# One layer of a gated-mixer decoder with mixture of experts: where the routing weights are applied, when the last down weights are requested, and which engine adds the token rows

## The chip, the cores and the metric

The kernel runs on one core of one Trainium2 chip. TensorE (PE) multiplies, VectorE (DVE), ScalarE (ACT) and GpSimd (POOL) do the rest, and SyncE (SP) requests nearly all transfers between HBM and SBUF; GpSimd requests those with a list of row numbers. The metric is the device time of one launch in microseconds (us), the median of several runs.

## The reference, cut to what matters

There are 512 tokens of 1024 channels, in float32. A first part (four gated mixers) is not touched by the change. The part that is:

```python
xn = rms_norm(x, ffn_norm_g)
# group = argmax of 4 group logits; two best of the 8 experts of that group
combine[token, expert] = p_group * top_p / sum(top_p)      # two non-zero values per token
for e in range(32):
    hid = silu(xn @ w_expert_gate[e]) * (xn @ w_expert_up[e])   # 1024 -> 256
    out = out + combine[:, e:e+1] * (hid @ w_expert_down[e])    # 256 -> 1024
return rms_norm(x + out, final_norm_g)
```

So each token gets its own row, plus two expert rows, each times a routing weight, and is then normalised.

## The kernel before

**Slots.** The 32 experts are handled in pairs. A pair fills 128 partitions: 64 slots for each of its two experts, and a slot holds one (token, expert) pair. Small tables made by TensorE from one-hot matrices `hot` give for each slot the row in which its result is kept (`slots`), its token (`toks`) and its token's norm factor (`rslot`). `weight_products` makes a table of the same kind for the routing weights, but of six columns only. There are 17 turns: the first four pairs (turns 0 to 3), three further pairs, two turns for the fullest expert, which gets more than 64 slots (`OVER`, `PART`), and the other eight pairs. Which pair holds the fullest expert is only known at run time, and so `exchange_columns` in turn 1 moves the columns of the tables about on VectorE, and `overflow_hits` then makes the matrices `hot` anew for the expert's slots beyond the 64th. These are chains of small operations, each of which waits for the one before.

**A turn.** TensorE multiplies 128 slots by the gate and up weights of both experts (line 2020, 64 matmuls), ScalarE and VectorE make `hid` from it (lines 1003 and 1552), TensorE transposes that (line 2040) and multiplies by the down weights (line 2061, 16 matmuls, two banks of PSUM `b` = 0 and 1). ScalarE and VectorE copy the banks to `ye` (lines 1021 and 1573), and GpSimd scatters the 128 rows to `y_dram`, which has two rows for each token (line 703).

**Weights.** Each turn needs six units of 1 MB. They lie in a ring of 20 slots; SyncE requests unit w as soon as unit w-20 has been used (`wait_reuse`), in the order of the turns. The last two units (the down weights of turn 16, `last_down`) are left out of this order: SyncE first waits for the 15 scatters, requests the results, and then the two units, in halves by columns, of which TensorE waits for the first with `d_half`.

**The end.** The last two turns (`KEPT`) do not go through `y_dram`. Their rows are split in two parts `yeh` and `yel` (ScalarE line 1012, VectorE line 1563; `w_kept` holds the routing weights of these two turns), and TensorE adds them to the tokens by a product with the one-hot matrices `pick` (`kept_products`, line 1977). The rows of the 15 other turns come back from `y_dram` in `load_results`, for each of the four tiles of 128 tokens two transfers of 0.5 MB (`yt[t][:, 0]` and `yt[t][:, 1]`, in the slots of `ring_z` and `ring_x`). VectorE multiplies them by the routing weights `cw` and adds the token's own row `x2` (`gather_results`, two operations per tile). For tiles 0 and 1 TensorE adds this to the sum in PSUM (`add_sum`, line 1985), for tiles 2 and 3 VectorE adds PSUM to it (`added`, line 1638). Then ScalarE squares and sums (line 1039), VectorE scales (`scaled`) and SyncE writes out. The tiles go in the order 3, 0, 2, 1 through TensorE (`SUMMED`) and 0, 3, 1, 2 through the norm (`NORMED`).

If an expert got more tokens than the two turns for it hold, the branches under `most > SLOT` run; with these inputs they do not.

## Time and profile before

| | |
|---|---|
| median of 3 runs | 736.96 us (734.79 to 739.46) |
| profiled execution | 735.92 us, of which the span of the trace is 734.2 us |
| mean granted TensorE clock | 0.975 of full speed |
| TensorE busy | 694.5 us (95%) |
| VectorE, ScalarE, GpSimd busy | 362.5, 252.2, 83.2 us |
| moved by DMA | 163.67 MB, mean 223 GB/s |
| turns 0 to 16 of the experts | from 478.6 to 718.5 us of the span |

The shares are averages over stages with different limits. In the part without experts (up to some 478 us) TensorE sets the time; in the expert part one has to look, stretch by stretch, whether TensorE or the stream of weights does; in the last 15 us neither is busy all the time.

### The profile page before, as it was taken

The numbers are of one execution on the slowest core, as the hardware profiler recorded it, in microseconds if no ns is written. First come the engines' busy times: TensorE is split into PE (matmuls) and PEld (weight loads), VectorE is DVE, ScalarE is ACT, GpSimd is POOL, SyncE is SP. The second block draws the span as 40 slices with busy tenths as digits, with TensorE's granted clock in tenths as the row PEclk, the third lists the DMA queues.
The fourth block names the chain that finished last, engine by engine and source line by source line (L and its number), as shares of the span: only waits on it lengthen the run. The fifth ranks groups of instructions, "written<-read, shape, count | busy, mean of one in ns | idle before, by whom it ended". The sixth has DMA issues, their size and how long they took to land.

```text
span 734.2 us, 9954 instructions
## 1 busy us (share of the span) xinstructions
PE 694.5 (95%) x3919; PEld 514.9 (70%) x3919; DVE 362.5 (49%) x700; ACT 252.2 (34%) x413; POOL 83.2 (11%) x117
## 2 busy tenths in 40 slices
PE   5999999999999999999999999699999999998975
PEld 4888987877777777788888888565555555554453
DVE  5378996356667767656456205635221212110246
ACT  7332135466767667544243211200010111110104
POOL 2001922000010101100002000201212121111000
PEclk9999999999999999999999999689999999998998
DMA  6523244221111122493405798489999999999982
GB/s 232 172 61 113 66 115 144 72 71 63 56 59 58 61 66 73 140 381 123 129 1 229 296 364 339 167 332 390 392 417 421 405 419 420 419 420 417 367 327 118
DMA packets 61153, 163.67 MB, mean 223 GB/s; under 512 B 7986, under 2 KB 39807, under 8 KB 49068
## 3 DMA queue, kind: packets, MB, share of 16 engines
q1 hardware_dynamic: 55468, 150.71, 54.3%
q0 software_dynamic: 5632, 12.25, 4.4%
q8 instruction: 33, 0.54, 0.3%
q14 instruction: 20, 0.16, 0.1%
HBM read 155.16 MB, written 15.99 MB: 233 GB/s over the span
## 4 chain that ended last, share of the span: by engine, by line
PE 82%; DMA 8%; DVE 4%; SPq 3%; ACT 2%; issue 1%; POOLq 0%; ACTq 0%; DVEq 0%
PE psum L1657 30%; PE psum L1753 12%; PE psum L2020 11%; PE psum L1932 6%; PE psum L2061 6%; DMA ring_z<-in_w_expert_up 4%; PE psum L1765 3%; SPq L495 2%; DMA ring_p<-in_w_expert_down 2%; PE psum L1778 2%; PE psum L1808 1%; DMA y_dram<-ye,slots 1%; PE psum L1843 1%; PE psum L1831 1%; PE psum L1891 1%
## 5 line engine op out<-in xcount | busy, mean ns | idle before, releaser
L1657 PE MATMUL psum<-xh,wh 128*128 128x512 f32 x256 | 99.9, 390 | 1.5 <-DVE xl L1049 1.5
L1657 PE MATMUL psum<-xh,wl 128*128 128x512 f32 x256 | 99.6, 389 | 0.0
L1657 PE MATMUL psum<-xl,wh 128*128 128x512 f32 x256 | 99.6, 389 | 0.0
L1052 DVE TENSOR_TENSOR wl<-raw,wh 128x1280 fp32r<-128x1280 f32 (+4 forms) x37 | 71.8, 1945 | 24.8 <-ACT wh L757 9.0
L1049 DVE SCALAR_TENSOR_TENSOR hid<-psum,rslot,act_g 128x256 f32<-128x256 f32 x17 | 8.2, 484 | 106.8 <-ACT act_g L1003 106.8
L1003 ACT ACTIVATE act_g<-psum,rslot 128x256 f32<-128x256 f32 x17 | 8.0, 473 | 149.9 <-PE psum L2020 149.9
L1657 PEld LDWEIGHTS psum<-xh,wh 128*128 128x128 f32 x256 | 48.1, 188 | 11.6 <-DVE xl L1049 1.7
L1657 PEld LDWEIGHTS psum<-xh,wl 128*128 128x128 f32 x256 | 48.1, 188 | 10.1
L1657 PEld LDWEIGHTS psum<-xl,wh 128*128 128x128 f32 x256 | 48.1, 188 | 9.8
L1753 PE MATMUL psum<-xh,wh 128*128 128x512 f32 x128 | 51.7, 404 | 0.0
L1753 PE MATMUL psum<-xh,wl 128*128 128x512 f32 x128 | 50.1, 391 | 0.0
L1753 PE MATMUL psum<-xl,wh 128*128 128x512 f32 x128 | 49.9, 390 | 0.0
L1049 DVE SCALAR_TENSOR_TENSOR sg<-cu,ch,sg 128x512 f32<-128x512 f32 x60 | 48.8, 883 | 0.0
L1573 DVE COPY ye<-psum 128x512 f32<-128x512 f32 x15 | 10.4, 692 | 60.7 <-PE psum L2061 60.7
L2020 PE MATMUL psum<-ring_h,xT 128*64 128x256 f32 x224 | 37.4, 398 | 3.1 <-DMA ring_h<-in_w_expert_up 3.1
L2020 PE MATMUL psum<-ring_w,xT 128*64 128x256 f32 x240 | 40.2, 379 | 0.0
L703 POOL DMA_INDIRECT y_dram<-ye,slots x15 | 15.1, 1008 | 172.9 <-DVE ye L1573 158.3
L2020 PE MATMUL psum<-ring_e,xT 128*64 128x256 f32 x160 | 31.3, 401 | 3.1 <-DMA ring_z<-in_w_expert_up 3.1
L2020 PEld LDWEIGHTS psum<-ring_h,xT 128*64 128x64 f32 x224 | 22.9, 143 | 14.2 <-issue 5.6
L2020 PE MATMUL psum<-ring_z,xT 128*64 128x256 f32 x128 | 31.8, 412 | 0.1
L2020 PEld LDWEIGHTS psum<-ring_w,xT 128*64 128x64 f32 x240 | 24.3, 137 | 8.9 <-issue 1.7
L1268 DVE TENSOR_TENSOR gp<-gs,psum 128x512 f32<-128x512 f32 x16 | 11.0, 685 | 36.6 <-PE psum L1657 35.8
(365 smaller groups left out, 1484.4 us busy)
## 6 DMA issues: line engine op xcount, KB each, us to landing
raw<-in_w_gate SPq DMA_DIRECT2D x16, 1024.0 KB, 6.3
raw<-in_w_in SPq DMA_DIRECT2D x9, 1024.0 KB, 5.8
ring_w<-in_w_expert_up SPq DMA_DIRECT2D x8, 1024.0 KB, 20.1
ring_w<-in_w_expert_gate SPq DMA_DIRECT2D x7, 1024.0 KB, 21.1
ring_h<-in_w_expert_gate SPq DMA_DIRECT2D x7, 1024.0 KB
ring_h<-in_w_expert_up SPq DMA_DIRECT2D x7, 1024.0 KB
ring_h<-in_w_expert_down SPq DMA_DIRECT2D x6, 1024.0 KB
ring_e<-in_w_expert_down SPq DMA_DIRECT2D x6, 1024.0 KB, 30.2
```

The costliest lines, as they stand in the source:

```text
L495: sp_e.dma_start(raw_slots[slot], weights(*units_of(c)[w], found)).then_inc(ring_full[slot], 16)
L703: pool.indirect_dma_start(out=y_dram[:, :], out_offset=bass.IndirectOffsetOnAxis(ap=slots[n, p], axis=0), in_=ye[n, s, :], in_offset=None, ...
L1049: return dve.scalar_tensor_tensor(out=out_, in0=a, scalar=s, in1=b, op0=o0, op1=o1)
L1052: return dve.tensor_tensor(dst, src, hi.bitcast(F32), ALU.subtract)
L1268: dve.tensor_tensor(gp[:, m, :], gs[:, m, :], branch_bank(cg, m)[:, :], ALU.mult).then_inc(S["gate_free"], 1)
L1657: last = nc.tensor.matmul(dst, a, b, start=start and n == 0, stop=stop and n == len(seq) - 1)
L1753: last = nc.tensor.matmul(bank[6 + n % 2][:, :], a[:, c, f], b[:, c, :], start=c == 0 and q == 0, stop=c == KC - 1 and q == 2)
L1765: last = nc.tensor.matmul(bank[4 + n % 2][:, :], a[:, j, f], b[g][:, j, :], start=j == 0 and q == 0, stop=j == BJ - 1 and q == 2)
L1778: last = nc.tensor.matmul(gate_bank(0, m)[:, :], a[:, c, f], b[:, c, :], start=c == 0 and q == 0, stop=c == KC - 1 and q == 2)
L1932: last = nc.tensor.matmul(bank[t][:, :], x_[:, t, c, :], w_[:, b, c, :], start=c == 0 and m == 0, stop=c == KC - 1 and m == 2)
L2020: last = nc.tensor.matmul(bank[2][half, m * FE:(m + 1) * FE], xT[:, k, half], w[h][:, k, :], start=k == 0 and m == 0, stop=k == KC - 1, sk ...
L2061: last = nc.tensor.matmul(bank[5 + b][half, :], hidT[:, m, half], w_d[h][:, m, b * T:(b + 1) * T], start=m == 0, stop=m == FE // P - 1)
```

## The change

Four things change. First, the routing weights are applied per slot when the down product leaves PSUM: the table of weights gets all 32 columns and becomes `wslot`, `slot_weights` copies it in turn 0, `exchange_columns` and `overflow_column` do for it what they do for `rslot`, and `weight_products` runs a second time in turn 1. `kept_weights` and `w_kept` go. Second, the last two down units are requested in their turn by the loop over all units, as whole units, ahead of the results. Third, GpSimd adds `x2` to the first of the two result rows of each tile (`add_tokens`), and VectorE adds the second (`add_rows`), one plain addition each. Fourth, the tiles go in the order 0, 2, 1, 3 through both TensorE and the norm; the square root's table on ScalarE is loaded in turn 16.

```diff
-        SUMMED, NORMED = (3, 0, 2, 1), (0, 3, 1, 2)
+        SUMMED = (0, 2, 1, 3)
 ...
-            last_down = [unit_no(0, LAST, half, 2) for half in range(2)]
-            for w in range(NU, last_down[0]):
+            for w in range(NU, UNITS0):
 ...
             load_results()
-            for w in last_down:
-                wait_reuse(0, w)
-            for b in range(2):
-                for w in last_down:
 ...
+            def add_tokens(n):
+                for t in range(NT):
+                    pool.wait_ge(y_in[t], 32 + 32 * n)
+                    pool.tensor_tensor(yt[t][:, 0, :], yt[t][:, 0, :], x2[:, t, :], ALU.add).then_inc(S["y_add"], 1)
+
             expert_pass(0)
+            add_tokens(1)
 ...
+                    if isinstance(c, int) and i == LAST:
+                        act.preload_act_table(ACT.Sqrt)
 ...
-                        act.activation(ye[:, s, 0:T], bank[5][:, :], ACT.Copy).then_inc(S["y_a"], 1)
+                        act.activation(ye[:, s, 0:T], bank[5][:, :], ACT.Copy, scale=wslot[:, column(c, i)]).then_inc(S["y_a"], 1)
 ...
+            def slot_weights(n):
+                dve.wait_ge(S["w_ps"], n)
+                for h in range(2):
+                    half = slice(h * SLOT, (h + 1) * SLOT)
+                    dve.tensor_copy(wslot[half, 0:NPAIR], bank[7][half, 448:448 + NE].rearrange("p (e h) -> p h e", h=2)[:, h, :]).then_inc(S["rs_ready"], 1)
 ...
-                exchanged(moved[:, FIXED:], rslot[:, FIXED:NPAIR], rslot[:, OVER:OVER + 1], gap[:, FIXED:])
-                one_column(bank[7][:, 384:384 + NE], emask)
-                st.mark(dve.tensor_copy(rslot[:, OVER:OVER + 1], rs[:, 13, 0:1]))
-                one_column(bank[7][:, 384:384 + NE], fmask)
-                st.link(dve.tensor_copy(rslot[first, NPAIR:NPAIR + 1], rs[first, 13, 0:1]))
+                for table, at in ((rslot, 384), (wslot, 448)):
+                    exchanged(moved[:, FIXED:], table[:, FIXED:NPAIR], table[:, OVER:OVER + 1], gap[:, FIXED:])
+                    one_column(bank[7][:, at:at + NE], emask)
+                    st.mark(dve.tensor_copy(table[:, OVER:OVER + 1], rs[:, 13, 0:1]))
+                    one_column(bank[7][:, at:at + NE], fmask)
+                    st.link(dve.tensor_copy(table[first, NPAIR:NPAIR + 1], rs[first, 13, 0:1]))
 ...
-            def gather_results(n, tiles):
-                for t in tiles:
-                    dve.wait_ge(y_in[t], 32 + 32 * n)
-                    for j, b in enumerate((x2[:, t, :], yt[t][:, 0, :])):
-                        stt(yt[t][:, 0, :], yt[t][:, j, :], cw[:, j, t:t + 1], b, ALU.mult, ALU.add).then_inc(S["comb_in"], 1)
+            def add_rows(n, t, done="comb_in"):
+                dve.wait_ge(y_in[t], 32 + 32 * n)
+                dve.wait_ge(S["y_add"], NT * (n - 1) + t + 1)
+                dve.tensor_tensor(yt[t][:, 0, :], yt[t][:, 0, :], yt[t][:, 1, :], ALU.add).then_inc(S[done], 1)
 ...
                     if isinstance(c, int) and i == 1:
                         exchange_columns()
-                        kept_weights()
                         overflow_hits()
 ...
-                    if isinstance(c, int) and i == LAST:
-                        gather_results(1, range(1))
 ...
-                                gather_results(1, range(1 + 2 * b, 3 + b))
+                                add_rows(1, b)
 ...
-                        dve.tensor_copy(ye[:, s, T:2 * T], bank[6][:, :]).then_inc(S["y_b"], 1)
+                        dve.tensor_scalar(ye[:, s, T:2 * T], bank[6][:, :], wslot[:, column(c, i)], None, ALU.mult).then_inc(S["y_b"], 1)
 ...
             expert_pass(0)
+            add_rows(1, 2)
 ...
-            added(3)
-            scaled(0)
-            scaled(3)
-            added(2)
-            scaled(1)
-            scaled(2)
+            scaled(0)
+            dve.wait_ge(S["comb_in"], 3)
+            added(2)
+            add_rows(1, 3, "comb")
+            dve.wait_ge(S["comb"], 2)
+            added(3)
+            for t in SUMMED[1:]:
+                scaled(t)
 ...
                     if isinstance(c, int) and i == 1:
                         pe.wait_ge(S["hot_ready"], NT + 1)
                         slot_products()
+                        weight_products()
                         norm_products(2)
```

VectorE in turn 1, from the last lookup in `slots` on. Before (`w_pairs` is the six-column table, `rc` a scratch table, L1468 the start of `overflow_hits`):

```order
L1457 TENSOR_SCALAR slots<-rs 64x1 [waits dve_step]
L1436 TENSOR_SCALAR rc<-rslot 128x12 [waits dve_step]
L1437 TENSOR_TENSOR rc<-rc 128x12 [waits dve_step]
...
L1463 COPY rslot<-rs 64x1 [waits dve_step]
L1512 COPY w_pairs<-psum 64x3 [waits dve_step,w_ps]
L1512 COPY w_pairs<-psum 64x3
L1436 TENSOR_SCALAR rc<-w_pairs 128x2 [waits dve_step]
L1437 TENSOR_TENSOR rc<-rc 128x2 [waits dve_step]
L1438 TENSOR_TENSOR w_pairs<-w_pairs,rc 128x2 [waits dve_step]
L1515 COPY w_kept<-w_pairs 128x2 [waits dve_step]
L1468 TENSOR_SCALAR rank<-rank 128x8 [waits dve_step]
L1344 TENSOR_SCALAR hot<-slot_no,rank 128x128 [waits rs_ps,dve_step]
```

Now, from the end of the same treatment of `rslot`:

```order
L1474 COPY rslot<-rs 64x1 [waits dve_step]
L1446 TENSOR_SCALAR rc<-wslot 128x12 [waits dve_step]
L1447 TENSOR_TENSOR rc<-rc 128x12 [waits dve_step]
L1448 TENSOR_TENSOR wslot<-wslot,rc 128x12 [waits dve_step]
L1452 TENSOR_TENSOR rc<-psum,rc 128x32 [waits dve_step]
L1453 TENSOR_REDUCE rs<-rc 128x1 [waits dve_step]
L1472 COPY wslot<-rs 128x1 [waits dve_step]
L1452 TENSOR_TENSOR rc<-psum,rc 128x32 [waits dve_step]
L1453 TENSOR_REDUCE rs<-rc 128x1 [waits dve_step]
L1474 COPY wslot<-rs 64x1 [waits dve_step]
L1479 TENSOR_SCALAR rank<-rank 128x8 [waits dve_step]
L1347 TENSOR_SCALAR hot<-slot_no,rank 128x128 [waits rs_ps,dve_step]
```

Between `rslot` and `rank` six small operations have become nine, all ahead of the matrices `hot`.

TensorE in turn 1, between the two halves of the turn. Before, and then now (L1958 and L1965 are `norm_products`, L1973 is `weight_products`):

```order
L1910 MATMUL psum<-rv,hot 128x32 [waits hot_ready]
L1910 MATMUL psum<-rv,hot 128x32 x7
L1958 MATMUL psum<-rro,hot 128x32 [waits rs_in]
L1958 MATMUL psum<-rro,hot 128x32 x7
```

```order
L1917 MATMUL psum<-rv,hot 128x32 [waits hot_ready]
L1917 MATMUL psum<-rv,hot 128x32 x7
L1973 MATMUL psum<-rvw,hot 128x32 [waits rs_in]
L1973 MATMUL psum<-rvw,hot 128x32 x7
L1965 MATMUL psum<-rro,hot 128x32 [waits rs_in]
L1965 MATMUL psum<-rro,hot 128x32 x7
```

Eight matmuls have come in, behind the wait for `hot` and ahead of the transposes of `hid`.

VectorE from the last `hid` on (turn 16). Before:

```order
L1049 SCALAR_TENSOR_TENSOR ring_z<-ring_z,cw,x 128x1024 [waits x0]
L1049 SCALAR_TENSOR_TENSOR ring_z<-ring_z,cw 128x1024 [waits comb_in]
L1049 SCALAR_TENSOR_TENSOR hid<-psum,rslot,act_g 128x256 [waits silu,comb_in]
...
L1049 SCALAR_TENSOR_TENSOR ring_x<-ring_x,cw 128x1024 [waits comb_in]
L1049 SCALAR_TENSOR_TENSOR yel<-psum,w_kept,yeh 128x512 [waits y_hi,comb_in]
L1049 SCALAR_TENSOR_TENSOR ring_x<-ring_x,cw,x 128x1024 [waits x3]
L1049 SCALAR_TENSOR_TENSOR ring_x<-ring_x,cw 128x1024 [waits comb_in]
L1049 SCALAR_TENSOR_TENSOR yel<-psum,w_kept,yeh 128x512 [waits y_hi,comb_in]
```

Now:

```order
L1052 SCALAR_TENSOR_TENSOR hid<-psum,rslot,act_g 128x256 [waits silu]
L1528 TENSOR_TENSOR ring_z<-ring_z 128x1024 [waits y_add,x0]
L1052 SCALAR_TENSOR_TENSOR yel<-psum,wslot,yeh 128x512 [waits y_hi]
L1528 TENSOR_TENSOR ring_z<-ring_z 128x1024 [waits y_add,x1]
L1052 SCALAR_TENSOR_TENSOR yel<-psum,wslot,yeh 128x512 [waits y_hi]
L1528 TENSOR_TENSOR ring_x<-ring_x 128x1024 [waits y_add,x2s]
```

Eight additions with a product have become four additions (that of tile 3 comes later, after `added(2)`), and each waits for GpSimd's `y_add`.

## Rows read from the trace of the kernel before

**Rows 1.** Windows: stretch, its length, busy time (instructions) by engine, TensorE clock, DMA share, GB/s.

```profile
515.00:520.00 5.00, 5.00 (x48) 3.18 (x45) 1.07 (x3) 0.28 (x1) 1.29 (x2) 1.00 0.91 321
520.00:525.00 5.00, 4.45 (x25) 2.02 (x25) 1.68 (x3) 1.17 (x3) 0.00 (x0) 1.00 1.03 420
...
684.00:688.00 4.00, 3.81 (x38) 3.08 (x38) 0.69 (x1) 0.00 (x0) 1.02 (x1) 1.00 1.00 416
...
692.00:696.00 4.00, 3.47 (x18) 1.46 (x19) 1.61 (x3) 0.88 (x2) 0.00 (x0) 1.00 0.67 259
```

**Rows 2.** Timeline of SyncE's requests: start, us, line, what, count.

```profile
519.78 0.33 SPq L495 DMA_DIRECT2D ring_h<-in_w_expert_gate  x1
...
670.32 2.58 SPq L495 DMA_DIRECT2D ring_h<-in_w_expert_up  x1
694.13 1.76 SPq L572 DMA_DIRECT2D ring_z<-y_dram  x4
...
698.20 6.31 SPq L584 DMA_DIRECT2D ring_p<-in_w_expert_down  x4
```

**Rows 3.** Who waited for whom, 640 us on: total, times, longest.

```profile
PE psum L2020 <- DMA ring_z<-in_w_expert_up: 3.1, 1, 3.1
```

**Rows 4.** Timeline of TensorE at the end; idle time before and its releaser in brackets.

```profile
700.18 8.81 PE L2020 MATMUL psum<-ring_h,xT 128*64 128x256 f32 x64 [3.07 <-DMA ring_h<-in_w_expert_up]
...
713.19 1.94 PE L2061 MATMUL psum<-ring_p,hidT 128*64 128x512 f32 x8 [0.63 <-DMA ring_p<-in_w_expert_down]
716.59 1.94 PE L2061 MATMUL psum<-ring_p,hidT 128*64 128x512 f32 x8 [1.46 <-DMA ring_p<-in_w_expert_down]
```

**Rows 5.** The chain that ended last, at the end: start, us, what.

```profile
720.44 3.66 PE psum L1977 x16
724.09 1.72 PE psum L1985 x4
...
726.77 1.12 ACT ring_z L1039 x2
728.44 1.28 DVE ring_z L1049
729.83 1.28 DVE ring_x L1049
```

**Rows 6.** Timeline of VectorE in turn 1.

```profile
498.96 0.23 DVE L1436 TENSOR_SCALAR rc<-rslot 128x12 f32<-128x12 f32 x1
...
500.59 0.14 DVE L1463 COPY rslot<-rs 64x1 f32<-64x1 f32 x1
...
501.92 0.17 DVE L1515 COPY w_kept<-w_pairs 128x2 f32<-128x2 f32 x1
```

**Rows 7.** The chain that ended last, in turns 0 and 1.

```profile
488.11 1.78 PE psum L1966 x16
...
505.11 1.80 PE psum L1958 x16
506.91 0.45 PE psum L2040 x2
```

**Rows 8.** Timeline of VectorE at the end.

```profile
702.54 1.28 DVE L1049 SCALAR_TENSOR_TENSOR ring_z<-ring_z,cw,x 128x1024 f32<-128x1024 f32 x1 [3.91 <-DMA ring_z<-y_dram]
...
719.70 0.75 DVE L1049 SCALAR_TENSOR_TENSOR yel<-psum,w_kept,yeh 128x512 fp32r<-128x512 f32 x1 [0.42 <-DVE ring_x L1049]
```

**Rows 9.** Line 572, the requests of the results: time from request to landing.

```profile
DMA to landing us min/median/max: 4.8/9.3/12.9
```

**Rows 10.** Timeline of GpSimd, two additions of the mixer part.

```profile
76.67 1.39 POOL L642 TENSOR_TENSOR axb<-axb,gs 128x512 f32<-128x512 f32 x1
...
87.04 3.43 POOL L642 TENSOR_TENSOR axb<-axb,gs 128x512 f32<-128x512 f32 x1
```

**Rows 11.** Timeline of VectorE beside the second of these.

```profile
87.03 2.28 DVE L1052 TENSOR_TENSOR wl<-raw,wh 128x2048 fp32r<-128x2048 f32 x1
```

**Rows 12.** Tile sg on VectorE: duration in ns, least, median, most.

```profile
L1049 DVE SCALAR_TENSOR_TENSOR sg<-cu,ch,sg x60: 737/744/1789, 43.4 to 112.3; 128x512 f32<-128x512 f32 x60
```

More of the change, by code:

```diff
@@ L1555, in expert_pass @@
                             x_out(E + 1, b)
+                    if isinstance(c, int) and i == 0:
+                        slot_weights(1)
+                        dve.wait_ge(S["rs_ready"], 4)
                     if isinstance(c, int) and i >= LAST - 1:
```

78 lines of the change are left out of this document (34 added, 44 removed).

## The prediction, made before the changed kernel was run

> **What bounds the kernel now.** I read four views in this order: the windows, to see stretch by stretch whether TensorE or the DMA is full; the waits, for who waits for a transfer; the chain that ended last; the timelines around the two places that the change touches, turn 1 and the end.
>
> The windows [rows 1] show two regimes. In the stretch 515 to 520 us the DMA is busy 0.91 of the time. From 520 to 688 us every stretch shows a share of 1.00 or more (24 stretches of 5 us to 640, twelve of 4 us to 688; the first and the last are shown). SyncE's request at 519.78 us takes 0.33 us, that at 670.32 us 2.58 us [rows 2]: the first finds an empty queue and had waited for a buffer, the second finds a full queue. So from 520 us on the stream of weights sets the pace, and TensorE, which is ahead by what the ring holds, runs into it twice, for 3.1 us each, before turns 14 and 16 [rows 3, 4]. **What counts for the expert part is when the stream gets the request of 519.78 us, and that hangs on TensorE in turns 0 to 2.** The two waits of 3.1 us are no reserve for a delay there, since they are waits for transfers that would be late by the same amount.
>
> At the end, SyncE requests nothing between 672.9 us (670.32 + 2.58) and 694.13 us, then the results, and the last down weights from 698.20 us on [rows 2]. The DMA share falls to 0.67 from 692 to 696 us [rows 1]. TensorE waits for the down weights before each half, 0.63 and 1.46 us, and is done with them at 718.53 us [rows 4]. A relay of TensorE, ScalarE and VectorE over four tiles follows; the last scaling ends at 731.1 us [rows 5], and the span ends 3.1 us later, with the last output.
>
> **The change, part by part.**
>
> *VectorE in turn 1.* The small operations on `rslot` run from 498.96 to 500.73 us [rows 6]; the same on `wslot` is new: 1.77 us. What goes is the work on the kept weights, from there to 502.09 us [rows 6]: 1.36 us. The matrices `hot` are ready 0.4 us later; I take 0.5, as one semaphore step is added too.
>
> *TensorE in turn 1.* It waits for `hot`, then runs slot and norm products, then transposes `hid` at 506.91 us [rows 7]; the chain goes straight from the norm products to the transposes, so `hid` is not what they wait for. A second set of weight products comes in between. That set, six columns wide, took 1.78 us in turn 0, and the norm products, already 32 wide, 1.80 us [rows 7]: the width costs nothing in turn 0, and the second set costs 1.8 us. The transposes start 0.5 + 1.8 = **2.3 us later**, and with them all of turns 1 and 2, the end of the gate and up product of turn 2, and the request of 519.78 us. Queued behind that request are all later weights, so the stream ends 2.3 us later. Bounds: nothing, if the stream had work left at 519.78; 2.8, if each of the nine new operations, and not only the first, takes the 0.23 us of rows 6. I take 2.3, as the request of 0.33 us speaks for an empty queue.
>
> *The rest of turns 0 to 15.* `slot_weights` are two small copies in turn 0, between `hid` and the down product, which VectorE waits for there; the three further operations of `overflow_column` stand likewise in turn 2 ahead of a `hid` that TensorE sets. The copies out of PSUM get a factor; with a factor and a second input they take 0.75 us [rows 8], and TensorE needs the bank again only a turn later. I cost this at nothing; the cover is VectorE's idle time, and without it three small operations cost 0.6 us.
>
> *The last down weights in their turn.* They are requested from 672.9 us on, right behind the weights of turn 16, whose landing starts that turn at 700.2 us [rows 4]. At 420 GB/s [rows 1] 2 MB take 5.1 us: they land at 705.3, before TensorE asks for them. Both waits for them go. TensorE is ready for them at 713.19 - 0.63 = 712.6, and two halves of 1.94 us [rows 4] end at 716.4 us in place of 718.5 (all times here still without the 2.3 us).
>
> *The results come later for it.* Before, tile 0 was used at 702.54 us, after a wait for its transfer [rows 8], and the last landed 12.9 us after its request, about 710 [rows 9]. Now 2 MB stand ahead on those of the DMA engines that are last: tile 0 at 702.5 + 5.2 = 707.8, then 2.5 us a tile, tile 3 at 715.3. Bounds: 702.5 for tile 0, if the share of 0.67 [rows 1] meant that all engines had time left, and 708.
>
> *GpSimd's additions.* The trace has none of 128x1024. Of two of 128x512, one took 1.39 us and one 3.43 us [rows 10]; the slow one ran beside a VectorE operation with two inputs from SBUF of 2.28 us [rows 11], and the sum of 1.39 and 2.28 is 3.67. VectorE's own operation on two SBUF rows took 744 ns at the median and 1789 at most [rows 12]. So they take turns rather than work side by side. Alone, twice 1.39 is 2.8 us for a tile; twice 3.43 is 6.9 at worst. I take 2.8 plus what VectorE holds. The page SBUF — State Buffer of the Trainium skill, section Who interferes with whom, says that of two such operations the second to issue "fully blocks"; rows 10 and 11 agree, and by that rule the tail is the slower of the two worked out next. The page GPSIMD Engine Reference, section 3, gives 4497 ns for an addition of 2048 columns, which makes an estimate of 2.25 us for 1024; by it GpSimd's four would be 2.2 us shorter together, and the tail the faster of the two.
>
> *The tail without blocking.* GpSimd ends tile 0 at 707.8 + 2.8 = 710.6, 1 at 713.4, 2 at 716.2, 3 at 719.0. `yel` was complete 1.9 us after TensorE's last half (720.45 after 718.53, [rows 4, 8]), so now at 718.3. TensorE needs 0.9 us for a set of four kept products (3.66 for four sets, [rows 5]) and has tile 0 at 719.2. Square and root, 1.5 us, and reciprocal with scaling, 1.4 (from 726.77 to 728.44, and 1.28, [rows 5]), end at 722.2. Then VectorE is the one that is busy: `added(2)`, `add_rows(3)`, `added(3)` at 1.3 each, three scalings at 1.4, to 730.3: **0.8 us earlier** than 731.1.
>
> *The tail with blocking.* From 707.8 us four additions of GpSimd and two of VectorE (1.3 each) follow each other before tile 3 is ready, 11.2 + 2.6, at 721.6. VectorE's addition for tile 2 ends at 722.9, `scaled(0)` at 724.3, and three times 1.3 and three times 1.4 lead to 732.4: **1.3 us later**. I take +0.6 between the two, nearer the row that shows blocking.
>
> Sum: 2.3 + 0.6 = 2.9 us. The profiled execution took 735.92 us and would take 738.8; it lies 1.04 us below the median of 736.96, so the median goes to **739.9 us**.
>
> **The rivals.**
>
> *A. The delay of turn 1 is absorbed.* If the stream still had work at 519.78, the 2.3 us vanish in the waits of 3.1 us and the tail alone counts. For it: a share of 0.91 is only 0.45 us of idle DMA. Against it: the request of 0.33 us. 736.96 with -0.8 to +1.3: 737.
>
> *B. GpSimd's additions end on the other side, clearly slower.* Each of the four meets an operation of VectorE as in rows 10 and costs 6.9 us: tile 3 is ready at 735.4, then `add_rows`, `added`, square with root, and scaling, 1.3 + 1.3 + 1.5 + 1.4, to 740.9: 9.8 us later than before, with the 2.3 us 749. It decides from about 4.5 us per addition on, where the sum reaches 1%. Against it: VectorE has only four such additions, of 1.3 us, to hold GpSimd up with.
>
> *C. The end gains more.* The down weights come early and the results not later, because the DMA had time left (share 0.67): tile 0 at 702.5 to 705, GpSimd is done before TensorE, and the tail gains the 2.1 us by which TensorE ends earlier. 736.96 + 2.3 - 2.1: 737; with A as well 734.9.
>
> **How the numbers follow.** Forecast 0.6, A 0.15, B 0.1, C 0.15 (0.04 of it with A). The range reaches from 736 (most of A and C) to 744.5 (the upper bounds 2.8 and 1.3, and GpSimd's four 0.9 us dearer each), and leaves out most of B and the far end of A and C, 2 in 10. One per cent, 7.4 us, is about what a measurement of this kernel can tell from no change. Faster by that, under 729.6, is more than any case gives: 0.02. Slower, over 744.3: B and the far end of the forecast, 0.13. Within: 0.85.
>
> **What would show it.** Turn 1: the transposes of `hid` at 509.2 us, line 1973 a second time, 1.8 us. The windows: the stretch that is not full reaches to 522 us. Turn 16 starts at 702.5 in place of 700.2. The end: TensorE does not wait for `ring_p`; GpSimd's four additions follow each other from some 710 us on, of 2.8 to 4.1 us each; `scaled(0)` comes behind VectorE's third `add_rows`. The prediction is wrong if turn 16 starts at 700 (A), if one addition takes over 4.5 us (B), or if tile 0 lands before 708 us with turn 1 late as said (C).

## The result

The changed kernel takes 739.68 us (median of 20 runs, 737.32 to 743.4), the kernel before in the same series 738.04 us (20 runs, 734.79 to 739.68). The medians are 1.6 us apart. The ratio over all runs of both is 1.0032 with a 95% interval of 1.0017 to 1.0047: 2.4 us slower, 1.3 to 3.5. The forecast was 739.9 us, made of +2.9 us and a median of three runs, 736.96 us, which lies 1.1 us under the 738.04 us of this series. The profiled execution took 739.98 us, with a span of 738.2 us. The difference of the two profiled executions, 4.1 us, is larger than that of the medians, mostly because that of before (735.92 us) lies 2.1 us under its median of 20 runs. So a size that one profile shows is not yet a size in time, and both are given where both are known.

### The profile page after: what moved, and what is told of

It is laid out like the page before. It is cut to its first block, busy times and chain, and to the rows that moved or that the text cites. A ratio compares the mean times of both kernels' runs of the same rounds, so it can differ in the third digit from the quotient of the medians.

```text
span 738.2 us, 9989 instructions
## 1 busy us (share of the span) xinstructions
PE 697.3 (94%) x3935; PEld 518.3 (70%) x3935; DVE 360.6 (49%) x702; ACT 253.5 (34%) x413; POOL 94.7 (13%) x121
## 4 chain that ended last, share of the span: by engine, by line
PE 86%; DMA 5%; DVE 4%; ACT 2%; SPq 1%; issue 1%; ACTq 0%; DVEq 0%; POOLq 0%
PE psum L1664 30%; PE psum L2027 13%; PE psum L1760 12%; PE psum L2063 7%; PE psum L1939 6%; DMA ring_h<-in_w_expert_up 4%; PE psum L1772 3%; PE psum L1785 2%; PE psum L1815 1%; SPq L494 1%; PE psum L2048 1%; PE psum L1850 1%; PE psum L1838 1%; PE psum L1898 1%; DVE hid L1052 1%
## 5 line engine op out<-in xcount | busy, mean ns | idle before, releaser
L1573 DVE TENSOR_SCALAR ye<-psum,wslot 128x512 f32<-128x512 f32 x15 | 11.3, 751 | 64.2 <-PE psum L2063 64.2
```

Source lines behind the costliest of these rows:

```text
L1573: dve.tensor_scalar(ye[:, s, T:2 * T], bank[6][:, :], wslot[:, column(c, i)], None, ALU.mult).then_inc(S["y_b"], 1)
```

## The profile after

**Turn 1.** The chain that ended last, in turn 1 of the changed kernel (start, us, what):

```profile
503.22 1.67 DVE hot L1347 x8
504.93 1.07 PE psum L1917 x8
506.00 2.23 PE psum L1973 x16
508.23 3.41 PE psum L1965 x16
511.65 0.49 PE psum L2048 x2
...
512.60 6.03 PE psum L2063 x16
```

Against [rows 7], the second set of weight products (line 1973) is there, as forecast, with 2.23 us. But the norm products behind it take 3.41 us where they took 1.80, and the down product takes 6.03 us. In the profile of before that down product is `507.82 4.88 PE L2061`, 16 matmuls; in turn 2 of both kernels it takes 3.65 us. From the end of the down product of turn 0 to the end of that of turn 1 it was 17.00 us before (495.70 to 512.70) and is 22.75 us now (495.88 to 518.63). The 5.75 us are: `hot` ready 0.70 us later, the new set 2.23, the norm products 1.61 more, the down product 1.15 more, gaps 0.06.

The windows of the changed kernel there, with busy time of TensorE, its weight loads, VectorE, ScalarE and GpSimd, then the granted clock, the DMA share and GB/s:

```profile
505.00:510.00 5.00, 5.00 (x34) 5.00 (x34) 1.93 (x5) 0.00 (x0) 0.00 (x0) 0.72 1.00 418
510.00:515.00 5.00, 4.53 (x16) 2.49 (x18) 0.00 (x0) 0.38 (x1) 0.00 (x0) 0.50 0.92 385
515.00:520.00 5.00, 5.00 (x28) 1.99 (x26) 1.21 (x5) 0.69 (x1) 0.00 (x0) 0.76 0.10 13
520.00:525.00 5.00, 5.00 (x50) 3.26 (x48) 2.43 (x11) 0.00 (x0) 2.02 (x2) 1.00 0.87 344
525.00:530.00 5.00, 4.45 (x28) 2.26 (x26) 1.68 (x3) 1.13 (x3) 0.00 (x0) 1.00 0.93 372
```

Two columns tell it. The clock falls from 1.00 to 0.72 and 0.50, which is the lower of its two levels, 1.2 GHz, while TensorE is busy for the whole of the first window. (Right ahead of it, until 504.93 us, it had waited 1.07 us for `hot`; before, 0.36 us. Experiment 3 shows that this wait is not what costs.) And the DMA share falls to 0.10 from 515 to 520 us, where it was 0.91 [rows 1]. The shares from 510 us on lack 0.08, 0.90, 0.13 and 0.07 of 5 us, together 5.9 us of idle DMA; before, 0.09 of 5 us, 0.45 us. So the stream of weights has lost 5.4 us. Before, SyncE's requests for the next gate weights came at 512.88 and 519.78 us, the second in [rows 2]; now they come later by 5.94 us each:

```profile
518.82 0.33 SPq L494 DMA_DIRECT2D ring_h<-in_w_expert_gate  x1
...
525.72 0.33 SPq L494 DMA_DIRECT2D ring_h<-in_w_expert_gate  x1
```

Most of the idle time, 4.3 us, lies between 514 us and the first of the two, when what had been requested earlier has landed.

**The end.** TensorE in turn 16, in the changed kernel:

```profile
705.84 8.46 PE L2027 MATMUL psum<-ring_h,xT 128*64 128x256 f32 x64 [3.06 <-DMA ring_h<-in_w_expert_up]
...
717.73 3.65 PE L2063 MATMUL psum<-ring_p,hidT 128*64 128x512 f32 x16
```

Turn 16 starts 5.66 us later than in [rows 4], behind the same wait of 3.1 us: the lost transfers arrive as a lost start, and no wait took them up. The two waits for the down weights are gone. The gate and up product takes 8.46 us here; in other profiles of this case it takes from 7.13 to 10.05 us, which matters for the end (see the table of stretches). GpSimd's four additions, and the times from request to landing of the results (line 570):

```profile
713.19 5.94 POOL L727 TENSOR_TENSOR ring_z<-ring_z,x 128x1024 f32<-128x1024 f32 x2 [22.10 <-DMA ring_z<-y_dram]
719.10 5.68 POOL L727 TENSOR_TENSOR ring_x<-ring_x,x 128x1024 f32<-128x1024 f32 x2
```

```profile
DMA to landing us min/median/max: 8.2/13.6/17.4
```

Tile 0 is there at 713.2 us, 7.35 us after the start of turn 16; the forecast had 7.6. Before, it was 2.4 us after it [rows 4, 8], and the landings took 4.8 to 12.9 us [rows 9]. An addition takes 2.9 us in the mean. VectorE at the end of the changed kernel:

```profile
715.67 1.23 DVE L1528 TENSOR_TENSOR ring_z<-ring_z 128x1024 f32<-128x1024 f32 x1 [0.28 <-POOL ring_z L727]
720.50 0.75 DVE L1052 SCALAR_TENSOR_TENSOR yel<-psum,wslot,yeh 128x512 fp32r<-128x512 f32 x1 [3.60 <-ACT yeh L1012]
...
723.12 2.74 DVE L1528 TENSOR_TENSOR ring_x<-ring_x 128x1024 f32<-128x1024 f32 x1
...
733.88 1.28 DVE L1052 SCALAR_TENSOR_TENSOR ring_x<-ring_x,stat,gfin 128x1024 f32<-128x1024 f32 x1
```

The addition at 723.12 takes 2.74 us where the one at 715.67 took 1.23: GpSimd's last one was running when it started, and it ends 1.08 us behind the end of that one. The last scaling ends at 735.16 us, 29.32 us after the start of turn 16; before it was 30.93 us. In this profile the end has gained 1.6 us, and the stretch ahead of it has lost 5.7.

## The experiments

Theory at the start: the second set of small products delays the request of 519.78 us and drags the clock down for what follows it; that is the whole loss, and the other edits are worth 0 to 1 us. Rival: the small products cost only their own time, and the rest comes from the end. A letter before each name says which kernel was edited, before (b) or after (a). Each was timed in five rounds, with the kernel before on the same chip (medians 737.4 to 737.7 us), except the last, which was only profiled.

### 1. The second set alone (b_narrow)

```diff
                         slot_products()
+                        weight_products()
                         norm_products(2)
```

> The kernel before with nothing but a second set of the eight narrow weight products (six columns) in turn 1; their result is not used. Theory 1 (the products cost their own 1.8 us): the transposes of hid in turn 1 at 508.7 us in place of 506.91, the down product of turn 1 still 4.9 us, turn 16 starts 1.8 us later, the time is 1.8 us (0.24%) over before. Theory 2 (the longer stretch of small products lets the granted TensorE clock fall to its lower level, and the norm products and the down product behind them pay for it): norm products near 3.4 us and the down product near 6 us, turn 16 starts 4 to 5 us later, the time is 4 to 5 us (0.6%) over before. Rival (the stream absorbs it): the transposes later, turn 16 at 700.2 us as before, no difference in time.

739.08 us, ratio 1.0020 (1.0002 to 1.0037). The chain in its turn 1, and the windows of TensorE (busy, clock, DMA share, GB/s):

```profile
508.90 1.78 PE psum L1966 x16
510.68 2.58 PE psum L1958 x16
...
514.21 5.68 PE psum L2062 x16
```

```profile
510.00:515.00 5.00, 4.53 (x27) 0.65 0.99 416
515.00:520.00 5.00, 5.00 (x20) 0.67 0.69 285
520.00:525.00 5.00, 5.00 (x50) 1.00 0.75 270
```

The set takes the forecast's 1.78 us here, yet the stretch from the slot products to the end of the down product grows from 8.65 to 12.05 us, by 3.4. The DMA is idle for 2.8 us in the last two windows, and from the end of the down product of turn 0 to turn 16 it takes 207.66 us against 204.48. So the second set alone, in the code of before, comes with a longer stretch at the lower clock and with a delay larger than its own time. The timed loss, 1.5 us (0.1 to 2.7), is smaller than the profile's 3.2, and by itself it would fit the 1.8 us of theory 1; the 4 to 5 us of theory 2 did not come. The profiled execution is the slowest of the twelve (742.84 us); of its distance to the profile of before, 3.5 us arose ahead of turn 0's small products, where the code is the same.

### 2. As long, but wide (b_wide)

```diff
                         slot_products()
+                        for m in range(2):
+                            nc.tensor.matmul(bank[3][:, :], ident[:, :], x2[:, m, 0:T], start=True, stop=True)
                         norm_products(2)
```

The products added here are two of 512 columns (four records in the trace), their result is not used, and they take as long as the narrow set.

> The kernel before with two wide float32 matmuls (identity by 512 columns, about 1.7 us together as the four records of line 1985 took, result unused) at the place where the second set of weight products stands in the changed kernel. Theory 1 (only their own time counts): as with the narrow set, turn 16 starts 1.7 us later. Theory 2 (it is the small products that let the clock fall): the wide ones hold the clock at its upper level, norm products at most 2 us, down product at most 4.9 us, turn 16 starts 1.2 to 1.7 us later, that is 2 to 3 us less delay than with the narrow set.

737.32 us, ratio 1.0002 (0.9983 to 1.0021). The chain in turn 1, and the windows of TensorE:

```profile
505.40 1.81 PE psum L2034 x4
507.21 1.71 PE psum L1958 x16
...
509.70 3.65 PE psum L2063 x16
```

```profile
505.00:510.00 5.00, 4.53 (x28) 1.00 0.99 413
510.00:515.00 5.00, 5.00 (x34) 1.00 1.07 423
```

This is the pair on which the argument rests. The same 1.8 us of TensorE at the same place, behind the same wait for `hot` (0.34 and 0.35 us): with narrow products the clock goes down to 0.65 and the down product takes 5.68 us, with wide ones it stays at 1.00 and the down product takes 3.65, which is less than in the kernel before (4.88). The whole stretch is 9.01 us against 8.65 in the first profile of before and 9.00 in the second: the kernel before already pays for its norm products in this way, and two wide products give back between 1.2 us and all of the 1.8 they cost. Turn 16 does not come later at all, where 1.2 to 1.7 us were expected. The times agree. The two kernels were timed in one series, twelve runs each; their medians are 1.8 us apart, their means 2.4 us, with 1.0 to 3.8 as my estimate of a 95% interval from these runs. The two sets differ in more than width, though: 16 matmuls and as many weight loads against 4. What of this the clock follows is not tested. The page "TensorE: Matmul & The Clock Gate" of the Trainium skill, section "HAM oscillation — how this bites in real kernels", explains a falling clock by idle gaps of TensorE. This pair shows something that such gaps don't explain: the gap ahead of the two sets is the same, and only behind the narrow set the clock falls. In the changed kernel, too, it falls in a window in which TensorE is busy for 5.00 of 5 us.

### 3. The change without its second set (a_no2nd)

```diff
                         slot_products()
-                        weight_products()
                         norm_products(2)
...
```

The edits left out here adapt VectorE's waits to this. The overflow slots get wrong weights here; the rest is the changed kernel.

> The changed kernel without the second set of weight products in turn 1 (the weights of the fullest expert's slots beyond the 64th are then wrong). Theory 2 (clock): the delay of turn 1 is only that of VectorE's chain, 0.9 us; norm products 1.8 us, down product 4.9 us; turn 16 starts at 701.1 to 702 us in place of 705.84, and the time is 3 to 5 us below the changed kernel, so 1 to 2 us below before, since the end of the changed kernel (from the start of turn 16) is 1.6 us shorter. Theory 1: 1.8 us below the changed kernel, 0.6 us over before.

736.14 us, ratio 0.9986 (0.9967 to 1.0005). Its turn 1 is that of before, with 1.80 us of norm products and this down product in the chain:

```profile
511.60 4.92 PE psum L2061 x16
```

TensorE still waits 1.05 us for `hot` here, as in the changed kernel, and the down product takes 4.92 us, as in the kernel before (4.88): the longer wait is not what makes it slow. From the end of the down product of turn 0 to turn 16 it takes 203.99 us (before 204.48). So all of the loss hangs on the second set. By time it is 1.0032 less 0.9986, 3.4 us. These are two series, and from their two intervals I estimate 1.6 to 5.2 us. All other edits together, the later `hot` among them, are worth 1.0 us, with an interval from 2.4 us gained to 0.4 lost.

### 4. The overflow work two turns later (a_late, b_late)

```diff
+                    if isinstance(c, int) and i == 3:
                         overflow_hits()
-                    if isinstance(c, int) and i == 2:
+                    if isinstance(c, int) and i == 4:
                         overflow_column()
...
-                    if isinstance(c, int) and i == 1:
+                    if isinstance(c, int) and i == 3:
```

The last `if` stands on TensorE, ahead of the slot, weight and norm products of the overflow column (in the kernel before: slot and norm products). The same edit was made in the changed kernel and in the kernel before.

> The changed kernel with the work on the overflow slots (overflow_hits, the second slot, weight and norm products, overflow_column, kept_rows) moved from turns 1 and 2 to turns 3 and 4. If turn 1 is where the change lost its time, and if from the request at the end of turn 2 on the stream of weights sets the pace, turn 1 and turn 2 lose nothing: in turn 1 no small products, down product 3.7 us, so the end of the down product of turn 1 comes about 5 us (before) to 10 us (changed) earlier after the hid of that turn than it did, as far as the stream has weights; turn 16 starts 5 to 7 us earlier than in the changed kernel. Together with the end, which stays: 5 to 8 us under the changed kernel, 3 to 5 us (0.4 to 0.7%) under before. Rival (the delay only moves along, since turns 3 and 4 still lie ahead of the point where the stream is the bound): no difference against the changed kernel.

> The kernel before with the same move (overflow work from turns 1 and 2 to turns 3 and 4). If small products in turn 1 cost before too (from the slot products to the end of the down product 8.65 us, of which 3.65 are the down product at the upper clock): turn 16 starts 3 to 5 us earlier, the time is 3 to 5 us (0.4 to 0.7%) under before. Rival: the stream is full anyway from 496 us on, at most the 0.45 us of idle DMA in 515 to 520 us are to be had, so 0 to 1 us.

The changed kernel with it takes 733.88 us, ratio 0.9947 (0.9930 to 0.9964), the kernel before with it 734.73 us, 0.9964 (0.9947 to 0.9982). Both beat both kernels: the changed kernel gains 5.8 us by the move (6.3 us by the ratios, since the kernel before took 0.65 us less in this series), the kernel before gains 2.7. The two are 0.85 us apart, with intervals that overlap, so this does not show that the rest of the change gains anything. In turn 3 the products of a_late still take 1.80 and 3.00 us with a down product of 5.22: the clock price is paid there too, and the stretch to turn 16 does not show it. Its turn 1, in the chain:

```profile
506.36 3.65 PE psum L2064 x16
```

The windows of b_late show why. From 510 us on the stream has work throughout:

```profile
510.00:515.00 5.00, 5.00 (x50) 1.00 1.02 398
515.00:520.00 5.00, 4.46 (x30) 1.00 1.00 407
520.00:525.00 5.00, 5.00 (x42) 1.00 1.02 428
```

From the down product of turn 0 to turn 16 it takes 203.27 us (a_late) and 203.14 (b_late), against 204.48 before and 209.96 after. So the kernel before had itself 1.3 us of such a delay.

### 5. The additions back on VectorE (a_dve_adds)

```diff
                 for t in range(NT):
-                    pool.wait_ge(y_in[t], 32 + 32 * n)
-                    pool.tensor_tensor(yt[t][:, 0, :], yt[t][:, 0, :], x2[:, t, :], ALU.add).then_inc(S["y_add"], 1)
+                    pass
...
                 dve.wait_ge(y_in[t], 32 + 32 * n)
+                dve.tensor_tensor(yt[t][:, 0, :], yt[t][:, 0, :], x2[:, t, :], ALU.add).then_inc(S["y_add"], 1)
```

> The changed kernel with both additions of each result tile on VectorE (1.2 to 1.3 us each), GpSimd does none. From the start of turn 16 to the last scaling the changed kernel took 29.3 us. Theory (GpSimd's additions of 2.9 us are hidden except where they hold VectorE's third addition up, 2.74 in place of 1.23 us): without them VectorE has four more operations, three of them before the first scaling, and wins the 1.5 us of the held-up addition: the end is 0 to 3 us later. Rival (contention costs more than the work moved away): 1 to 2 us earlier.

741.17 us, ratio 1.0050 (1.0032 to 1.0067). Beside the changed kernel's 1.0032 that is 1.3 us, which the two intervals don't separate for certain. The profile has 32.05 us from the start of turn 16 to the last scaling against 29.32. So GpSimd's part in the change is not the loss that rival B had; a gain of that order is likely, but not shown.

### 6. The results ahead of the down weights (a_results_first)

```diff
-            for w in range(NU, UNITS0):
+            for w in range(NU, UNITS0 - 2):
...
             load_results()
+            for w in range(UNITS0 - 2, UNITS0):
+                wait_reuse(0, w)
+                load_unit_no(w, 0, found)
```

> The changed kernel with the last two down units requested after the results, as before, but as whole units. The part up to turn 16 stays. Theory (the end hangs on TensorE's last down product, GpSimd's additions are hidden): the first result tile comes 2.3 us after the start of turn 16 in place of 7.4, GpSimd is done with all four before the down product, VectorE's additions of 1.2 us are not held up, but TensorE waits for the down weights until about 16.5 us after the start of turn 16 and ends 20 us after it in place of 15.5: the last scaling comes 1 to 3 us later than in the changed kernel. Rival (GpSimd's late additions are what sets the end): 1 to 2 us earlier.

744.66 us, ratio 1.0103 (1.0079 to 1.0126): 5 us worse than the changed kernel. GpSimd has its first tile 2.4 us after the start of turn 16 (703.59), and TensorE waits:

```profile
706.03 2.36 POOL L730 TENSOR_TENSOR ring_z<-ring_z,x 128x1024 f32<-128x1024 f32 x1 [18.76 <-DMA ring_z<-y_dram]
708.55 2.35 POOL L730 TENSOR_TENSOR ring_z<-ring_z,x 128x1024 f32<-128x1024 f32 x1 [0.16 <-DMA ring_z<-y_dram]
```

```profile
718.99 4.30 PE L2066 MATMUL psum<-ring_p,hidT 128*64 128x512 f32 x12 [3.36 <-DMA ring_p<-in_w_expert_down]
```

The last scaling comes 34.56 us after the start of turn 16 against 29.32, 5.2 us later where 1 to 3 were expected. Whole down units behind the results cost 3.4 us of waiting, and the down product behind that wait takes 5.35 us in place of 3.65, with a granted clock of 0.53 from 720 to 722 us. The wait was expected, the slower product was not. The kernel before has the same order, with the units in halves by column. It waits 0.63 and 1.46 us [rows 4] and its down product takes 3.88 us, so it is spared 1.3 us of waiting and 1.5 us of the slower product.

### 7. The down weights in turn, alone (b_down, b_down2)

```diff
-            for w in range(NU, last_down[0]):
+            for w in range(NU, UNITS0):
...
             load_results()
-            for w in last_down:
-                wait_reuse(0, w)
-            for b in range(2):
...
-                        pe.wait_ge(S["d_half"], 32)
```

> The kernel before with one part of the change alone: the last two down units are requested in their turn, as whole units, ahead of the results. The expert part is as before (turn 16 at 700.2 us). Theory 1 (the results come about 5 us later, and four tiles of two operations each on VectorE are then the end): TensorE no longer waits for the down weights, its last half ends at 716.2 to 716.4 us, but the first result tile comes at 707 to 708 us in place of 702.5, and VectorE's eight products and sums of 1.3 us run behind hid, end no earlier than 720 us; the end is 0 to 2 us later than before. Theory 2 (what counts is TensorE's end of the down product): 2 us earlier.

> The kernel before with the last two down units in turn, a second time. If the first timing (ratio 0.998) stands, 0.5 to 2 us under before; if the profile's tail stands (32.5 us from the start of turn 16 to the last scaling against 30.9), 0 to 2 us over it.

736.66 us, ratio 0.9982 (0.9966 to 0.9997), and the second time 737.59 us, 0.9992 (0.9973 to 1.0011). The two together say no more than that it gains 0 to 2 us, where I had expected a loss of 0 to 2. The tails of the profiles (start of turn 16 to last scaling) are 32.54 and 31.19 us, against 30.93 and 31.31 in the two of before, so they show no gain. TensorE's down product waits for no transfer, but it waits for `hid`, which stands on VectorE behind the first gathering of tile 0. VectorE in b_down2:

```profile
711.00 1.28 DVE L1039 SCALAR_TENSOR_TENSOR ring_z<-ring_z,cw,x 128x1024 f32<-128x1024 f32 x1 [9.57 <-DMA ring_z<-y_dram]
712.32 1.28 DVE L1039 SCALAR_TENSOR_TENSOR ring_z<-ring_z,cw 128x1024 f32<-128x1024 f32 x1
713.64 0.48 DVE L1039 SCALAR_TENSOR_TENSOR hid<-psum,rslot,act_g 128x256 f32<-128x256 f32 x1
```

`hid` comes two operations after a wait of 9.57 us. In the changed kernel that addition is GpSimd's, and `hid` comes first. So I take the two edits to belong together: later results need a VectorE that does not stand in line for them. A kernel with the down weights in turn and only the order on VectorE changed was not run.

### 8. The first set moved too (b_late2, b_late2_down)

```diff
                         exchange_columns()
+                    if isinstance(c, int) and i == 3:
                         kept_weights()
...
                         slot_products()
+                    if isinstance(c, int) and i == 2:
                         weight_products()
```

This is on top of b_late; b_late2_down has the edit of experiment 7 as well.

> The kernel before with the overflow work in turns 3 and 4, and now also the first weight_products moved from turn 0 to turn 2 (kept_weights to turn 3). Theory (a small-product set in the first turns costs its own 1.78 us and slows the down product behind it, 5.35 us against 3.65 us in a turn without one, and the delay is carried to the end because weight requests then come late): a further 3.5 us under the run with the overflow work moved alone (734.7 us), so about 731.5 us, 5.5 to 6.5 us under before; the down product of turn 0 at 3.65 us. Rival (the stream is full from turn 0 on, so that TensorE's earlier end is waited away at a later weight): no difference to 734.7 us, with a TensorE wait of some 3 us more before turn 4.

> The same as the run beside it, and the last two down units requested in turn, whole, ahead of the results. Theory (from the timed run of that edit alone, 1.3 us under before): 1 to 1.5 us under the run beside it, TensorE without a wait at the last down product. Rival (from the profile of that edit alone, in which the last scaling came 1.6 us later after the start of turn 16): 0 to 1.6 us over it, because VectorE waits for the results of tile 0, which stand ahead of hid in its order.

734.59 us, ratio 0.9963 (0.9947 to 0.9980), and 734.44 us, 0.9954 (0.9939 to 0.9970). Both are b_late's 734.73 again: I had expected 3.5 us more, which the intervals exclude. The rival is the nearer one, though the wait of 3 us before turn 4 that it named is not in the trace. The edit of experiment 7 on top makes 0.15 us, which speaks for neither of the two forecasts about it. In the profile the down product of turn 0 did go from 5.35 to 3.65 us, but the stretch from there to turn 16 grew from 203.14 to 204.76 us. That took back 1.6 of 3.5 us: counted from the slot products of turn 0, turn 16 starts after 210.28 us in place of 212.10. So the profile leaves 1.8 us gained, of which the times show nothing. The stream had work in all of that stretch. The windows of b_late2:

```profile
490.00:495.00 5.00, 4.74 (x28) 1.00 1.01 423
495.00:500.00 5.00, 5.00 (x48) 1.00 1.00 401
500.00:505.00 5.00, 4.46 (x28) 1.00 1.03 417
```

So the same kind of delay costs its full length in turn 1 with a second set, by the profiles, and half of it or nothing in turn 0.

The two kernels have the same small products in turns 2 and 3, and their profiles still differ there. First b_late2, with its weight products in turn 2, then b_late2_down in the same turn, and behind slot and norm products in turn 3:

```profile
515.00:520.00 5.00, 4.53 (x22) 0.67 1.01 418
```

```profile
515.00:520.00 5.00, 4.53 (x28) 1.00 1.03 426
...
530.00:535.00 5.00, 4.53 (x28) 1.00 1.02 417
```

The down product of turn 2 takes 5.14 us in one and 3.65 in the other. So one narrow set does not bring the clock down in every execution. In turn 1, slot and norm products alone did it in all five profiles that have them there without a further set, and with a second narrow set in all four.

### 9. The kernel before, profiled again (before_again)

> The kernel before, profiled a second time: the stretch from the end of the down product of turn 1 to the start of turn 16 within 1 us of 187.5, the last stretch within 1 us of 30.9; the down product of turn 1 at 4.9 us. If these differ by more, single profiles can't carry differences of that size.

One execution, 736.91 us. The stretch from the down product of turn 1 to turn 16 is 187.19 us (187.48 in the first profile) and the tail 31.31 us (30.93), both within the 1 us expected. But the down product of turn 1 was not at its 4.9 us, so a single profile can't carry a difference of 0.5 us in it:

```profile
508.27 5.35 PE psum L2061 x16
```

### The stretches side by side

In us, from the profiles. TensorE's end is that of its last down product.

| Kernel | Slot products to end of down, turn 1 | End of down, turn 0, to turn 16 | Turn 16 to TensorE's end | Of this, gate and up product | From there to the last scaling |
|---|---|---|---|---|---|
| before | 8.65 | 204.48 | 18.35 | 8.81 | 12.58 |
| before_again | 9.00 | 204.52 | 18.72 | 7.13 | 12.59 |
| b_narrow | 12.05 | 207.66 | 18.27 | 7.13 | 12.60 |
| b_wide | 9.01 | 204.02 | 18.31 | 7.13 | 12.58 |
| b_down | 8.98 | 204.66 | 18.71 | 7.13 | 13.83 |
| b_late | – | 203.14 | 17.16 | 7.13 | 12.83 |
| after | 13.70 | 209.96 | 15.54 | 8.46 | 13.78 |
| a_no2nd | 8.67 | 203.99 | 17.13 | 10.05 | 14.24 |
| a_late | – | 203.27 | 15.89 | 8.81 | 15.53 |
| a_dve_adds | 13.70 | 209.39 | 15.82 | 8.75 | 16.23 |
| a_results_first | 12.03 | 207.17 | 20.75 | 8.54 | 13.81 |

The second column follows the first, kernel by kernel. The last three show the trade of the end: the changed end brings TensorE 1.2 to 2.8 us ahead of the first profile of before, and the relay behind it takes 1.2 to 3.0 us longer. They also show something that I had not looked for. Without waits for the down weights, TensorE's end comes 7.1 us behind the end of the gate and up product of turn 16, in all four kernels with the changed end and order (after, a_no2nd, a_late, a_dve_adds), and that product takes from 8.46 to 10.05 us:

```profile
702.80 10.05 PE L2026 MATMUL psum<-ring_h,xT 128*64 128x256 f32 x64 [3.05 <-DMA ring_h<-in_w_expert_up]
```

Behind that wait of 3.05 us the granted clock is 0.50 from 702 to 708 us. Where the clock is at 1.00 behind the same wait, as in before_again from 700 us on, the product takes 7.13 us. In the kernel before it makes no difference to the end, since TensorE then waits for the down weights: 30.93 us from the start of turn 16 to the last scaling with a product of 8.81 us, 31.31 with one of 7.13.

## Why the prediction came out

**The number was right, and two errors of opposite sign in its sum are why it came out so close: the term for turn 1 was less than half of what the profile showed, and the rest came out lower by the times than the loss that was forecast.** Term by term:

*The place: right in the main.* The delay of turn 1 reached the end through late weight requests, and the waits before turns 14 and 16 took up nothing. DMA idle time (5.4 us more) and start of turn 16 (5.7 us later) agree. But 4.3 of the 5.9 us of idle time lie ahead of the request before the one named, that of 512.88 us, now at 518.82: the stream ran dry one request earlier than I had it. Rival A falls for turn 1, with 209.96 us against 204.48, and experiment 3 shows it by time. In turn 0 rival A's mechanism holds at least in part (experiment 8).

*The size in turn 1: the step that failed.* It reads "the width costs nothing in turn 0, and the second set costs 1.8 us", and gives 2.3 us with bounds of 0 and 2.8. The profile has 5.75 us there, outside the bounds. The new set's own time and the later `hot` make 2.9 of that; the other 2.8 us are norm and down products that ran at the lower clock behind it. The transposes of `hid`, forecast for 509.2 us, start at 511.65. What would have shown it was in the trace: in turn 1 of before the clock already fell, and its down product took 4.88 us where that of turn 2 took 3.65. I priced the added instructions and not what they did to the ones behind them. Experiments 1 and 2 show that it is the narrow products, and not 1.8 us of TensorE. By time the second set alone is 3.4 us in the changed kernel (1.6 to 5.2) and 1.5 in the kernel before (0.1 to 2.7), for a forecast 1.8; the profile has 5.05 without the later `hot`. So the times alone do not prove the term too small; the profiles do. They explain some of the distance: the stretch takes 13.70, 13.70 and 12.03 us in three kernels with the same turn 1, so one execution doesn't fix it. The rest stays open.

*VectorE in turn 1:* 0.5 us was taken, the profile has 0.7 for `hot`.

*The down weights in turn: right for TensorE.* It waits for no transfer and takes 15.54 us to its end; the forecast was 716.4 - 700.18 = 16.2. (2 MB at 420 GB/s are 5.0 us, not the 5.1 and 5.2 that I used; nothing hangs on it.) Within the changed kernel this order is worth 5 us against whole units behind the results (experiment 6), but against the halves of before it is worth 0 to 2 us (experiment 7), since it moves the wait to the results.

*The results later: right*, tile 0 at 7.35 us after the start of turn 16 for a forecast 7.6. That refutes rival C, whose gain rested on results that come no later.

*GpSimd's additions: right in size.* I took 2.8 us alone; it is 2.35 and 2.36 where VectorE is idle (experiment 6) and 2.9 in the mean in the changed kernel. The estimate of 2.25 us from the figure in the page "GPSIMD Engine Reference" of the Trainium skill, section 3, was closer than mine from rows. Rival B's 6.9 us never came; the longest was 3.44. Its limit of 4.5 us per addition does not follow from its own terms either: they give 2.5 us in all there, and reach 1% only at 5.7.

*The tail: not settled.* I took +0.6 us between -0.8 and +1.3. The profile of the changed kernel has -1.6 (29.32 against 30.93), outside these bounds, but the same end in a_no2nd and a_late takes 31.37 and 31.42 us, +0.4 and +0.5. By time all edits but the second set make -1.0 us (-2.4 to +0.4). Two things differ between these profiles. One is the clock in turn 16: the gate and up product takes 1.6 us more in a_no2nd than in the changed kernel, 0.35 more in a_late. The other is where GpSimd's additions meet VectorE's. The relay of a_late is 1.75 us longer than that of the changed kernel, and in it TensorE waits 1.46 us for the second `yel`. In a_late the meeting falls between the two operations on `yel` that TensorE waits for:

```profile
715.59 0.75 DVE L1052 SCALAR_TENSOR_TENSOR yel<-psum,wslot,yeh 128x512 fp32r<-128x512 f32 x1 [3.95 <-ACT yeh L1012]
716.26 3.34 DVE L1528 TENSOR_TENSOR ring_z<-ring_z 128x1024 f32<-128x1024 f32 x1
719.52 0.74 DVE L1052 SCALAR_TENSOR_TENSOR yel<-psum,wslot,yeh 128x512 fp32r<-128x512 f32 x1
```

```profile
713.85 4.67 POOL L727 TENSOR_TENSOR ring_x<-ring_x,x 128x1024 f32<-128x1024 f32 x2
```

VectorE's addition takes 3.34 us in place of 1.23, and the second `yel` is 2.1 us late. In the changed kernel's profile the same addition (721.16) took 1.38 us, and the one held up came after `yel`. I expected them to block each other, as the page "SBUF — State Buffer" of the Trainium skill, section "Who interferes with whom", says. The traces agree closely. In the four profiles with GpSimd's additions, six of VectorE's additions ran beside one of GpSimd's that had started first, and each ended 1.08 or 1.09 us behind it. Five of GpSimd's had started behind one of VectorE's, and each ended 2.21 to 2.24 us behind that one. I did not ask which instruction of VectorE would be the one held.

*Not tested:* the order of the tiles (0, 2, 1, 3) by itself, the moved load of the activation table, and the factors in the copies out of PSUM. Together with everything else but the second set they make the 1.0 us of experiment 3.

*The sum:* +2.9 us forecast; by time, 3.4 for the second set and -1.0 for all the rest, 2.4 us. The forecast had 1.8 for the second set and 1.1 for the rest, 0.5 of it for the later `hot`. Two errors of opposite sign, +1.6 and -2.1 us, cancelled for the most part, and that is luck. So is the closeness of 739.9 to 739.68 us: with the base of this series, 738.04 us, the same +2.9 would have read 740.9. With the overflow work two turns later the changed kernel takes 733.88 us, and the kernel before 734.73.

## What to carry to other kernels

Before adding small matmuls to a stretch, look at the granted clock there and price the large matmuls behind them at the lower level too. Then find the window from which the DMA share stays at 1.00. Here a delay before it that let the share fall arrived in full at the last turn in the profile (5.75 and 5.66 us), and the same work behind it cost nothing that the times show. And where a transfer is moved forward, see which one it pushes back, and what stands behind that one's first reader on its engine.

## What the runs showed of the hardware

- The granted clock of TensorE fell to 0.50 behind sets of 16 matmuls of 6 or 32 columns, while TensorE was busy without a gap. With wide matmuls of the same duration at the same place it was 1.00 in the one profile taken, and a down product of the same shape took 3.65 us behind the wide set, 4.88 to 5.35 in turn 1 behind the norm products alone and 5.07 to 6.03 behind two narrow sets. In one profile (b_late2_down) single narrow sets left the clock at 1.00.
- The same narrow set took 1.78 us in one kernel and 2.23 in another, the norm products 1.71 to 3.41.
- Behind a wait of 3.1 us for a transfer, the same gate and up product took from 7.13 us (granted clock 1.00) to 10.05 us (0.50 for its first 5 us).
- A GpSimd addition of 128x1024 in f32 took 2.35 and 2.36 us with VectorE idle; a VectorE addition of that shape, 1.21 to 1.23 alone, took up to 3.34 us beside one of GpSimd's that had started first, and ended 1.08 or 1.09 us behind it each time.
